# The first feed-forward matrix by seven block products in place of eight, in 18 of its 22 weight units

## What is computed

```python
gate, up = jnp.split(h @ w_ffn_in[l], 2, axis=-1)      # h: 512 x 1024, w_ffn_in[l]: 1024 x 5632
f = (jax.nn.silu(gate) * up) @ w_ffn_out[l]            # w_ffn_out[l]: 2816 x 1024
```

## Time and profile before

| | |
|---|---|
| time, median of 3 runs | 4039.99 us (4036.91 to 4041.23) |
| the profiled execution | 4035.31 us, its span 4033.6 us |
| PE busy | 3723.9 us, 92% |
| DVE busy | 1960.3 us, 49% |
| ACT busy | 1240.5 us, 31% |
| granted PE clock, mean | 0.957 |
| DMA | 319.42 MB, 79 GB/s |

### The profile page before, as it was taken

One profiled execution on the slowest core, in us unless ns is written; L12 is line 12 of the kernel. 1 busy time (PEld: TensorE's weight loads), 2 busy tenths in 40 slices (PEclk: granted clock), 3 DMA queues, 4 the chain that ended last, 5 costly groups with the idle time before them and its releaser, 6 DMA issues.

```text
span 4033.6 us, 44530 instructions
## 1 busy us (share of the span) xinstructions
PE 3723.9 (92%) x15715; PEld 2866.9 (71%) x15715; DVE 1960.3 (49%) x2509; ACT 1240.5 (31%) x1487; POOL 79.0 (2%) x67
## 2 busy tenths in 40 slices
PE   5889998787999699999899999989999979999998
PEld 4556887555788588877467778878887746777886
DVE  6545432654443434537656544334443766654433
ACT  3433222343222222223442322222222343232222
POOL 1000000100000000000000000000000000000000
PEclk8989999898999899999799999999999989999999
DMA  3111222111222222232113322222223211322221
GB/s 117 68 42 63 94 91 86 60 63 42 83 94 94 73 84 94 91 91 76 48 32 84 94 94 94 89 90 83 94 93 96 73 45 42 84 94 86 94 96 57
DMA packets 343678, 319.42 MB, mean 79 GB/s; under 512 B 11032, under 2 KB 336868, under 8 KB 343524
## 3 DMA queue, kind: packets, MB, share of 16 engines
q1 hardware_dynamic: 339316, 307.94, 24.3%
q0 software_dynamic: 2560, 8.26, 0.6%
q10 hardware_dynamic: 1648, 1.34, 0.1%
HBM read 315.40 MB, written 2.10 MB: 79 GB/s over the span
## 4 chain that ended last, share of the span: by engine, by line
issue 55%; PE 39%; DVE 3%; ACT 1%; POOL 1%; DMA 0%; DVEq 0%; ACTq 0%; POOLq 0%
PE products L627 35%; PE products L831 1%; POOL mean_sq L2270 1%; PE small L702 1%; DVE X L1560 0%; PE products L721 0%; ACT w_hi L1112 0%; DVE xT L1674 0%; PE small L900 0%; PE small L670 0%; DVE a_lo L1584 0%; DMA sinks<-in_sink 0%; PE small L783 0%; PE products L920 0%; PE products L712 0%
## 5 line engine op out<-in xcount | busy, mean ns | idle before, releaser
L627 PE MATMUL products<-a_hi,w_hi 128*128 128x512 f32 (+1 forms) x3152 | 1276.6, 405 | 112.7 <-DVE a_lo L1584 86.4
L627 PE MATMUL products<-a_lo,w_hi 128*128 128x512 f32 (+1 forms) x3152 | 1262.7, 401 | 0.0
L627 PE MATMUL products<-a_hi,w_lo 128*128 128x512 f32 (+1 forms) x3152 | 1261.9, 400 | 0.0
L1112 ACT ACTIVATE w_hi<-raw 128x2048 fp32r<-128x2048 f32 x302 | 578.5, 1916 | 2015.9 <-PE products L627 2015.8
L1536 DVE TENSOR_TENSOR w_lo<-raw,w_hi 128x2048 fp32r<-128x2048 f32 x302 | 691.4, 2290 | 648.6 <-ACT w_hi L1112 647.8
L627 PEld LDWEIGHTS products<-a_hi,w_hi 128*128 128x128 f32 (+1 forms) x3152 | 600.0, 190 | 289.0 <-DVE a_lo L1584 95.9
L627 PEld LDWEIGHTS products<-a_lo,w_hi 128*128 128x128 f32 (+1 forms) x3152 | 601.1, 191 | 148.4 <-issue 3.9
L627 PEld LDWEIGHTS products<-a_hi,w_lo 128*128 128x128 f32 (+1 forms) x3152 | 600.3, 190 | 149.1
L1551 DVE TENSOR_TENSOR X<-products,rs 128x1024 f32<-128x1024 f32 x178 | 216.8, 1218 | 908.1 <-PE products L627 907.0
L627 PE MATMUL products<-h_hi,w_hi 128*128 128x512 f32 x1056 | 418.6, 396 | 0.0
L627 PE MATMUL products<-h_hi,w_lo 128*128 128x512 f32 x1056 | 418.6, 396 | 0.0
(11 more groups left out here) (318 smaller groups left out, 2757.6 us busy)
## 6 DMA issues: line engine op xcount, KB each, us to landing
raw<-in_ffn_w SPq DMA_DIRECT2D x240, 512.0 KB, 4.3
raw<-in_w_in SPq DMA_DIRECT2D x104, 512.0 KB, 4.6
raw<-in_w_ffn_in SPq DMA_DIRECT2D x88, 512.0 KB, 4.3
raw<-in_w_out SPq DMA_DIRECT2D x32, 512.0 KB, 4.0
raw<-in_w_ffn_out SPq DMA_DIRECT2D x32, 512.0 KB, 4.2
raw<-in_ffn_w SPq DMA_DIRECT2D x32, 384.0 KB, 3.6
raw<-in_w_ffn_out SPq DMA_DIRECT2D x16, 384.0 KB, 3.5
raw<-in_w_mem_kv SPq DMA_DIRECT2D x8, 512.0 KB, 4.0
```

Of the source, the lines that this page charges most:

```text
L627: mm = pe.matmul(G[pair][0:m, into + b, 0:n], w[:, s, at:at + m], x, start=(first or into > 0) and k == 0 and q == 0, stop=(last or ends) ...
L1112: act.activation(w_hi[:, s, :], raw[:, s, :], ACT.Copy).then_inc(hi_ready, 1)
```

## The change

The first matrix of every feed-forward part keeps 4 plain units (2 pairs, `N_PLAIN = 2`). The other 18 units (`N_SEVEN`) are each cut into four quarters: the weights A into 512 input channels by 128 output channels, the moving operand B into 512 input channels by 256 tokens. The four quarters of the result come from seven products in place of eight (the form of Strassen's method with 15 additions). Each product is 4 chunks x 3 = 12 matmuls of 256 columns. The loop is written out: 18 units x 84 matmuls stand in the program of PE, three times.

What is new around them:

- DVE makes from B, once for each feed-forward part and in float32, the eight quarters and combinations (`halves`, then T1, T3, T2, T4), now already scaled by `rs`; ACT and DVE split seven of them (`half_high`, `half_low`), so that no result need be scaled.
- For each unit v, DVE makes four sums of weight quarters (`first_sums`: S3, S2; `other_sums`: S4, S1), ACT makes the high parts (A11 with A12, S3 with S2, S1 with S4, A22) and DVE the low ones. The calls for unit v+1 stand among those of unit v.
- PSUM adds: P1, then P6 on top, then P5, then P3, all in one bank. ACT copies the bank after each of the four (`copied`, 128x256) into a quarter of the result; P7 goes through a tile of its own; DVE adds P7, P4 and P2 to the quarters (`with_p7`, `with_p4`, `with_p2`). P6 waits for the copy of P1, P4 for that of P7, P5 for that of P6, P3 for that of P5.
- Silu and the product of gate and up (`gated`) work on whole tiles in `h_full`. The split into `h_hi` and `h_lo` (`high_of_h`, `low_of_h`) is put off: their space holds B's parts until the last unit is done. The second matrix waits for it pair by pair, and runs both blocks of a chunk one behind the other.
- In `piece`, wherever `fresh` is used, the order becomes chunk by chunk, both blocks in turn.

```diff
-                for b, (m, terms) in enumerate(blocks):
-                    if b == 1 and between:
+                order = [(b, k) for b, (_, terms) in enumerate(blocks) for k in range(len(terms))]
+                if fresh or pairs is not None:
+                    order.sort(key=lambda at: at[1])
+                for b, k in order:
+                    m, terms = blocks[b]
+                    at, hi, lo = terms[k]
+                    if between and (b, k) == (1, 0):
                         between()
...
+            def seven():
...
+                for v, name in SEVEN_ORDER:
+                    slot, pair = (first_unit + v) % 2, (first_group + v) % 2
+                    if name == "P1":
+                        w, x, out, starts = "A11", "B11", z_bank(pair), True
+                        pe.wait_ge(form_lo, at["form_lo"] + 3 * v + 1)
...
+                    elif name == "P6":
+                        w, x, out, starts = "S2", "T2", z_bank(pair), False
+                        pe.wait_ge(part_copied, at["part_copied"] + COPY_AT[v, "P1"])
+                    elif name == "P4":
+                        w, x, out, starts = "A22", "T4", y_bank(pair), False
+                        pe.wait_ge(part_copied, at["part_copied"] + COPY_AT[v, "P7"])
+                        pe.wait_ge(lo_ready, c.next("lo_ready"))
...
+                    for k in range(4):
+                        cut, part = slice(k * P, (k + 1) * P), slice(k * HALF, (k + 1) * HALF)
+                        for q, (ww, xx) in enumerate(((wh, xh), (wh, xl), (wl, xh))):
+                            mm = pe.matmul(out, ww[:, cut], xx[:, part], start=starts and k == 0 and q == 0,
...
+                for v in range(N_SEVEN + 2):
...
+                    if 1 <= v <= N_SEVEN:
+                        copied(v - 1, "P5", out_quarter(v - 1, 1, 1), z_bank(1 - pair))
+                    if v < N_SEVEN - 1:
+                        high_aa(v + 1)
...
+                    if v < N_SEVEN:
+                        if v % 2 == 0:
+                            act.wait_ge(h_ready, at["h_ready"] + max(N_PLAIN, v // 2))
+                        copied(v, "P1", out_quarter(v, 0, 0), z_bank(pair))
+                    if v < N_SEVEN - 1:
+                        high_sums("SS", v + 1, 1)
...
+                        copied(v, "P7", p7_tile(v), y_bank(pair))
...
+                for v in range(N_SEVEN):
...
+                        first_sums(v + 1)
+                    if v:
+                        with_p7(v - 1)
+                    if not last:
+                        low_aa(v + 1)
+                    if v == 0:
+                        half_low("B22")
+                    elif v % 2 == 0:
+                        gated(v - 1)
+                    if not last:
+                        other_sums(v + 1)
+                        low_sums("SS", v + 1, 2)
...
+                    with_p4(v, pair)
+                    if not last:
+                        low_sums("S1S4", v + 1, 3)
+                        low_a22(v + 1)
...
+                    with_p2(v, pair)
```

More of the change, by code:

```diff
@@ L237 @@
 RANKS = ((3, 4), (0, 1, 2))
+N_PLAIN = 2
+N_SEVEN = 2 * (FC // 2 - N_PLAIN)
+SEVEN_ORDER = [(v - (name == "P3"), name) for v in range(N_SEVEN + 1)
+               for name in ("P1", "P7", "P3", "P6", "P4", "P2", "P5")
+               if (v < N_SEVEN or name == "P3") and (v or name != "P3")]
+SEVEN_AT = {key: n + 1 for n, key in enumerate(SEVEN_ORDER)}
+N_PRODUCTS = len(SEVEN_ORDER)
+COPY_AT = {key: n + 1 for n, key in enumerate(key for key in SEVEN_ORDER if key[1] not in ("P4", "P2"))}
+LAST_USE = ("P1", "P1", "P7", "P7", "P6", "P6", "P4", "P4", "P2", "P5", "P3")
@@ L612, in take_unit, with piece @@
                 c.unit += 1
-            def piece(blocks, first=True, last=True, n=SEQ, fresh=None, between=None, signals=True, into=0, ends=False):
+            def piece(blocks, first=True, last=True, n=SEQ, fresh=None, between=None, signals=True, into=0, ends=False,
+                      pairs=None):
                 s = (c.unit - 1) % 2
@@ L676, in ffn @@
                 full(between=spread)
-                for _ in c.turns(pe, 1, FF // (2 * P), PER_TURN["ffn_in"], "ffn_in"):
+                for _ in range(2 * N_PLAIN - 2):
                     full()
-                    full()
-                pe.wait_ge(hl_ready, c.next("hl_ready", FF // (2 * P) - 1))
-                c.one("hl_ready")
+                seven()
+                pairs = c.now("hl_ready")
+                c.one("hl_ready", FC // 2)
                 for _ in c.turns(pe, 0, 2, PER_TURN["ffn_out"], "ffn_out"):
@@ L685, in ffn @@
                             take_unit()
[L686 to L688 removed]
+                            tall(nk, 2 * P, h_hi, h_lo, k0=k0, first=k0 == 0, last=k0 == 16, pairs=pairs + k0 // 2)
                 if post_norm:
@@ L1172, in ffn @@
                     operand(gain, l, squares)
-                def gate_and_up(i):
-                    unit_done()
-                    group_read()
-                    act.activation(X[:, 0:2, :], X[:, 0:2, :], ACT.Silu).then_inc(silu_ready, 1)
-                    unit_done()
-                    group_skipped()
-                    act.wait_ge(h_ready, c.next("h_ready"))
-                    c.apart(act)
-                    act.activation(h_hi[:, bass.ds(i * 2, 2), :], X[:, 2:4, :], ACT.Copy).then_inc(hh_ready, 1)
-                gate_and_up(0)
-                for i in c.turns(act, 1, FF // (2 * P), PER_TURN["ffn_in"], "ffn_in"):
-                    gate_and_up(i)
+                seven()
                 if between:
@@ L1349, in positions @@
             def positions():
-                act.wait_ge(hl_ready, c.next("hl_ready", FF // (2 * P)))
+                act.wait_ge(h_ready, c.now("h_ready"))
                 c.apart(act)
```

402 lines of the change are left out of this document (355 added, 47 removed).

## The result

| | before | after |
|---|---|---|
| time, median | 4038.7 us, 4 runs (4036.9 to 4041.2) | 3947.2 us, 4 runs (3946.0 to 3949.3) |
| ratio, 95% interval | | 0.9774 (0.9757 to 0.9791) |
| profiled execution, span | 4035.3, 4033.6 us | 3947.9, 3945.9 us |
| mean granted PE clock | 0.957 | 0.946 |

A forecast was written before the change was run, and what follows sets the result against it. PE was taken as the bound, busy 3723.9 of 4033.6 us. Terms -148.6 + 48.9 + 3 + 10 - 7.8 + 3.3 = -91.2 us bring the profiled 4035.3 to 3944.1, median 3949 us; range 3920 to 4010.

The forecast's parts named there:

- waits and first distances: Start of the seven products, six feed-forward parts: PE waits cost +48.9 us, longer first matmul distances after them +3.
- entries of the second block: Where `fresh` waited 3.14 and 0.78 us, chunk-by-chunk order removes both waits, each there twice: -7.8 us.
- first block's feed-forward entries: First block's two feed-forward parts: PE comes earlier, waits nearly 4 us, and the clock may dip: +3.3 us.
- The gain on PE: Seven-product units: 84 matmuls at 0.1175 us take 9.87 instead of 11.25 us; 108 units give -148.6 us.
- DVE's pace: Steady seven-product units: DVE needs 8.3 to 8.6 us of 9.87, so it keeps up and costs nothing.
- The rival's 10.2: Rival, seven-product units: waits cost DVE 0.12 us per operation, it needs 10.2 us and sets the pace; 4002 us, chance 0.13.
- the five waits: PE waits where the seven products begin: 0.8, 3.2, 3.2, 0.3 and 0.65 us, 8.15 us per feed-forward part.
- the walk: Operation-by-operation timing of DVE, ACT and PE where the seven products begin, giving 8.15 us of PE waits per part.
- one dip of 1.66: PE's clock at 0.50 after gaps at the seven's start: 1.66 us, once per feed-forward part, +10.0 us in all.
- wait 3: First seven-product unit: P4 waits for the copy of P7 on ACT, starting 3.2 us after P6.
- Chunk order: Chunk-by-chunk order where `fresh` is used: -7.8 us from waits removed, +3.3 us in the first block's feed-forward parts.
- PE's instruction stream: Rival, at 756 product starts: each 0.1 us costs 76 us, 4100 at 0.2; chance 0.09 slower, 0.06 mild but faster.

The follow-up runs named there:

- both runs: Changed kernel with 9 instead of 12 matmuls per product: 3797.9 us; changed kernel computing the low part of A11 and A12 twice in 17 units: 3946.6 us.

## Why the prediction was right

The terms of the sum, beside what the profiles show (the spans differ by 87.7 us):

| term | forecast | measured | how |
|---|---|---|---|
| 108 units | -148.6 | -140.7 | 108 x (11.25 - 9.947) |
| waits and first distances | +51.9 | +44.9 | what is left of the six stretches (-82.1) without the lines above and below |
| clock in the feed-forward parts | +10.0 | +13.7 | changed kernel against the one with filled gaps |
| entries of the second block | -7.8 | -12.0 | 2 x 4.94 and 1.02 + 1.04 |
| first block's feed-forward entries | +3.3 | +5.9 | 2.98 + 2.92 |
| first block's entries behind the sums over `zmT` | 0 | -5.6 | 2 x (12.81 - 10.02) |
| elsewhere | 0 | +6.1 | remainder |
| sum | -91.2 | -87.7 | |

The total came out 3.5 us from the forecast with single terms off by up to 8; that they cancel so well is luck.

**The gain on PE.** Right in kind, 8 us too large: 117.5 ns was read from products with one pair of tiles, and P4, P5 and P3 have another. The term that was mis-sized is the distance of 256-column matmuls: 118.4 on the mean. The rule of the Trainium skill at full clock ("TensorE: Matmul & The Clock Gate", section "Back-to-back issue gap", given there for a single matmul by itself; 109.2 and 215.8 ns) was not reached by any layout here: 116.7 and 226.7 were the best. The distances in the forecast lay 7.6 and 8.6% above it, not 9.

**DVE's pace.** Right. 8.3 to 8.6 us was worked out, at most 8.56 measured, and in the changed kernel DVE waits for PE. The rival's 10.2 is excluded by both runs.

**The start of the seven.** Four of the five waits stood where the walk had put them, ended by what it had named. In size, by the brackets: 0.4 for 0.8, 2.6 for 3.2, 1.8 for 3.2, none for 0.3, 0.5 for 0.65. The third was too long because the walk left P6 at full clock, though the next paragraph of the prediction had the clock fall there. Read from start to start, with P6 at full clock and the first distance in it, the four cost 0.70, 2.82, 3.14 and 0.73 us, 44.3 in six parts, which fits the 44.9 of the table.

**The clock.** The step "one dip of 1.66, as the second half of a double one falls into wait 3" had the mechanism, and the size only by luck. The low clock lasted through P6, P4 and P2, 3.8 us of slowness in the third part, of which P6's 1.15 were hidden; in four parts of the kernel with the old order it lasted a third of that.

**Chunk order.** Both signs right, both sizes low: the gap of 3.14 us also took slow matmuls behind it, and at the first block the dip cost 3 in place of 1.66. A third place was overlooked, the entries behind the sums over `zmT`, whose -5.6 us nearly make up for the first block's +5.9.

**PE's instruction stream.** The first matmul of a product follows the last one at the usual distance: 1458.46 + 1.41 = 1459.87 in the chain. The 0.22 us of the earlier trace rows comes only after a gap. No fetch gap shows either, though the page has 150 in place of 76 packets of instructions in its first such queue. One reading in the argument against this rival was wrong: of the eight one-column matmuls in the earlier trace rows the second to the eighth start 0.112 us apart, not 0.094, so that the slack worked out from it is 0.07 us a product, not 0.28. That none was needed is shown by the chain. What nobody had forecast is the place of the tiles, which weighs as much as the algorithm.

## What to carry to other kernels

Before you count on fewer or shorter matmuls, read the distance of the present ones for every pair of weight and operand tiles: here a pad of 96 bytes was worth 2.3%, and the best offset for 512 columns was the worst for 256. A new pipeline pays where it starts: write down which queue serves its first unit in which order, and see whether a wait is the order's or a backlog's. Here gaps of 2.6 and 1.8 us on PE, close together, cost themselves and up to 10 us at half clock; matmuls whose result nobody uses, set into the gaps, bought the clock back at no cost. When an order is changed, list every place that uses it: here one was missed that was worth 5.6 us.

## What was not expected of the hardware

- The distance of matmuls depends on where the two tiles begin: 226.7 to 234.3 ns for 512 columns, 116.7 to 120.2 for 256.
- The low clock behind the same pair of gaps lasted about 10 us in one part of a kernel and 3 to 4 in another.
- 20 matmuls of 256 columns in a gap (2.53 us) keep the clock at 1.00.
- The mixing stretches move by some 3 us between kernels whose code there is the same (from the spread at 776 us to the channel sums at 980, 204.4 us in the kernel before and 207.4 in the changed kernel with the old order); it was not followed up.
